# A hybrid recurrent and mixture-of-experts layer on one core: router logits beside the output projection, norms by quarters, the first four experts written out, chunk states on two halves of the rows

## The reference

```python
mod = silu(c) @ ada_w + ada_b                     # six shifts, scales and gates per sequence
h = rmsnorm(x, n1) * (1 + sc1) + sh1
z = h @ w_in                                      # HGRN2 and GLA operands, merge gates ma, mb
o_h, s_h = gated_linear_recurrence(...)           # 4 heads, 128 x 128 state
o_g, s_g = gated_linear_recurrence(...)           # 4 heads, 64 x 128 state
merged = sigmoid(ma) * (o_h @ w_bh) + sigmoid(mb) * (o_g @ w_bg)
x = x + gt1 * (merged @ w_out)
h2 = rmsnorm(x, n2) * (1 + sc2) + sh2
logits = h2 @ r_w + r_b                           # 32 experts, top 4, softmax over these
x = x + gt2 * sum_e combine[:, e] * (swiglu(h2 @ w_gu[e] + b_gu[e]) @ w_dn[e] + b_dn[e])
y = rmsnorm(x, final_g)
```

## Time and profile before

| what | us |
|---|---|
| median of three runs | 1472.11 |
| the profiled execution | 1469.54 |
| its span (first to last instruction) | 1467.5 |
| TensorE matmuls busy | 1311.6 (89%) |
| VectorE / ScalarE / GpSimd busy | 518.3 / 274.4 / 35.1 |
| mean DMA rate over the span | 321 GB/s |
| mean granted TensorE clock | 0.939 of full |

### The profile page before, as it was taken

The page is one execution under the profiler, slowest core; times in us unless marked ns, Lnnn a source line. Parts: engine busy times, 40 slices in busy tenths (PEclk is TensorE's granted clock), DMA queues, the critical chain, the costliest instruction groups (busy, mean ns, idle before and its releaser), DMA issues.

```text
span 1467.5 us, 29078 instructions
## 1 busy us (share of the span) xinstructions
PE 1311.6 (89%) x11811; PEld 595.9 (41%) x11812; DVE 518.3 (35%) x1159; ACT 274.4 (19%) x517; POOL 35.1 (2%) x50
## 2 busy tenths in 40 slices
PE   4999999999978997978787999897999779899996
PEld 1656576666743332323132333232333223243332
DVE  4143334233483332323133344231433223243436
ACT  2130013000011221211011222121222112122222
POOL 0000000000000000000000000000000000000003
PEclk8999999989988999989798999998999989899997
DMA  9877341305275999999999999999799999998830
GB/s 388 311 304 304 113 165 58 117 17 190 83 286 228 409 412 412 416 419 418 419 416 418 418 418 417 416 419 418 283 401 409 411 416 419 418 419 355 328 129 36
DMA packets 87450, 470.92 MB, mean 321 GB/s; under 512 B 7984, under 2 KB 8000, under 8 KB 51360
## 3 DMA queue, kind: packets, MB, share of 16 engines
q1 hardware_dynamic: 84416, 460.68, 77.2%
q0 software_dynamic: 2432, 7.75, 1.9%
q10 hardware_dynamic: 576, 2.11, 0.4%
HBM read 465.66 MB, written 4.85 MB: 321 GB/s over the span
## 4 chain that ended last, share of the span: by engine, by line
PE 72%; DMA 17%; SPq 5%; DVE 3%; issue 2%; ACT 1%; DVEq 0%
PE bank L927 21%; DMA ring<-in_exp_w_dn 12%; PE bank L656 12%; PE bank L944 11%; SPq L451 4%; PE bank L896 4%; PE bank L882 4%; PE bank L793 2%; PE bank L823 2%; PE bank L654 2%; PE bank L903 2%; DMA arena<-in_exp_w_gu 2%; DMA ring<-in_ada_w 2%; DMA ring<-in_exp_w_gu 2%; ACT arena L1178 1%
## 5 line engine op out<-in xcount | busy, mean ns | idle before, releaser
L927 PE MATMUL bank<-arena 128*32 128x512 f32 x1984 | 249.2, 640 | 46.2 <-DMA arena<-in_exp_w_gu 46.0
L944 PE MATMUL bank<-ring,arena 128*32 128x256 f32 x3584 | 219.3, 382 | 33.1 <-ACT arena L1178 18.6
L1621 DVE TENSOR_SCALAR arena<-bank 128x256 f32<-128x256 f32 x56 | 23.8, 425 | 569.2 <-PE bank L927 569.2
L927 PE MATMUL bank<-ring,arena 128*32 128x512 f32 x1600 | 190.8, 622 | 19.0 <-DMA ring<-in_exp_w_gu 19.0
L1615 DVE TENSOR_TENSOR gates<-gates,bank 128x1280 f32<-128x1280 f32 x112 | 166.7, 1488 | 92.7 <-PE bank L896 92.7
L656 PE MATMUL bank<-arena,ring 128*128 128x320 f32 (+1 forms) x592 | 177.4, 461 | 2.7 <-DVE arena L1253 2.0
L944 PEld LDWEIGHTS bank<-ring,arena 128*32 128x32 f32 x3584 | 105.5, 109 | 131.1 <-issue 54.0
L656 PEld LDWEIGHTS bank<-arena,ring 128*128 128x128 f32 (+1 forms) x592 | 117.3, 201 | 66.6 <-issue 25.1
L927 PEld LDWEIGHTS bank<-arena 128*32 128x32 f32 x1984 | 56.3, 112 | 214.3 <-DMA arena<-in_exp_w_gu 106.5
L1175 ACT ACTIVATE arena<-arena 128x256 f32<-128x256 f32 x56 | 23.4, 417 | 459.1 <-DVE arena L1621 459.1
L927 PEld LDWEIGHTS bank<-ring,arena 128*32 128x32 f32 x1600 | 48.3, 112 | 141.8 <-issue 97.7
(11 more groups left out here) (259 smaller groups left out, 926.1 us busy)
## 6 DMA issues: line engine op xcount, KB each, us to landing
ring<-in_exp_w_gu SPq DMA_DIRECT2D x128, 1024.0 KB, 20.2
ring<-in_exp_w_dn SPq DMA_DIRECT2D x128, 1024.0 KB, 11.0
arena<-in_exp_w_gu SPq DMA_DIRECT2D x128, 1024.0 KB, 19.5
ring<-in_ada_w SPq DMA_DIRECT2D x24, 1024.0 KB, 21.1
ring<-in_w_in SPq DMA_DIRECT2D x20, 1024.0 KB, 10.2
ring<-in_w_out SPq DMA_DIRECT2D x4, 1024.0 KB, 7.3
ring<-in_w_in SPq DMA_DIRECT2D x4, 528.0 KB, 10.3
arena<-in_state_hgrn POOLq DMA_DIRECT2D x4, 512.0 KB, 7.8
```

Of the source, the lines that this page charges most:

```text
L927: last = mm(out[part(g), :, :], h2g[:, chunk(k)], w[:, :, columns(g)], start=False, stop=(k == DC - 1), tile_position=(0, CAP * g))
L944: last = mm(banks[2][part(g), HALF:2 * HALF], actT[:, chunk(k)], pair(item_slot(DC + k // 2))[:, k % 2, columns(g)], start=(k == 0), stop= ...
```

## The change

Line numbers of the changed program differ; the names of functions and tiles are kept.

**Chunk states on two halves.** `vmask` has two chunks of columns instead of four. TensorE multiplies rows 0 to 63 and rows 64 to 127 apart, each as a tile of 64 rows, and the two write different banks; `chunk_state(c)` says where chunk `c` is found.

```diff
-                            last = mm(bU[p][p0:p0 + dk, :], kdtok[:, p, p0:p0 + dk],
-                                      vmask[bi][p].rearrange("p c v -> p (c v)"), start=True, stop=True)
+                            for x in range(2):
+                                last = mm(bU[x][p0:p0 + dk, p * 2 * P:(p + 1) * 2 * P], kdtok[64 * x:64 * x + 64, p, p0:p0 + dk],
+                                          vmask[bi][p][64 * x:64 * x + 64, :, :].rearrange("p c v -> p (c v)"),
+                                          start=True, stop=True, tile_position=(64 * x, p0))
```

```diff
+                TS(hT[:, f, 0:TP], xT[:, f, 0:TP], modT[:, 32 + f, 0:1], None, ALU.mult)
+                TT(hT[:, f, TP:T].rearrange("p (b t) -> p b t", t=TSQ), xT[:, f, TP:T].rearrange("p (b t) -> p b t", t=TSQ),
+                   modT[:, 32 + f, 1:NROW].unsqueeze(2).broadcast_to([P, NSEQ, TSQ]), ALU.mult).then_inc(u_scaled, 1)
...
+                if f == 3:
+                    pe.wait_ge(router_landed, 32)
+                    b = open_turn("lsh")
+                    for k in range(DC):
+                        mm(b[0:NROW, 0:E], modT[:, 24 + k, :], rw[:, k, :], start=(k == 0), stop=False)
+                    mm(b[0:NROW, 0:E], ones[0:1, 0:NROW], rb, start=False, stop=True).then_inc(turn_filled, 1)
+                    for n in range(3):
+                        raw_logits(n)
+                elif f > 3:
+                    raw_logits(f - 1)
+            raw_logits(DC - 1)
```

```diff
+            def quarter_sums(b, src, start, stop):
+                for g in range(4):
+                    ins = mm(b[CH * g:CH * g + CH, 0:QT], ones[:, 0:CH], src[:, g * QT:(g + 1) * QT], start=start, stop=stop,
+                             tile_position=(0, CH * g))
...
-            step(nc.vector.reciprocal(r0, r0))
-            dve.wait_ge(router_landed, 32)
-            modulate(32, 24, h2_ready, False)
+            nc.vector.reciprocal(r4, r4).then_inc(r4_ready, 1)
+            wait_filled(dve, "spread3")
+            TT(logT.rearrange("p (g t) -> p g t", g=4), logT.rearrange("p (g t) -> p g t", g=4), upper[0:E, :, 0:QT], ALU.mult)\
+                .then_inc(logits_scaled, 1)
+            for k in range(0, DC, 2):
+                by_quarter = hT[:, k:k + 2, :].rearrange("p k (g t) -> p k g t", g=4)
+                TT(by_quarter, by_quarter, upper[:, :, 0:QT].unsqueeze(1).broadcast_to([P, 2, 4, QT]), ALU.mult)\
+                    .then_inc(h2_scaled, 1)
```

```diff
+            wait_taken(pe, TURN["place"])
+            _, first = nc.values_load_multi_w_load_instructions(itemtab[0:1, 0:5], engines=[mybir.EngineType.PE],
+                                                                min_val=0, max_val=NI - 1)
             pe.wait_ge(comb_ready, 1)
...
-            with pe.Fori(0, E // 4) as fours:
+            for x in range(4):
+                with pe.Fori(first[x], first[x + 1]) as i:
+                    item(i, x // 2, x % 2)
+            with pe.Fori(1, E // 4) as fours:
```

```diff
-            for f in range(6):
-                ins = STT(xT[:, f, :], xT[:, f, :], V("final")[:, f:f + 1], r0, ALU.mult, ALU.mult)
+            for f in range(DC):
+                ins = STT(xT[:, f, :].rearrange("p (g t) -> p g t", g=4), xT[:, f, :].rearrange("p (g t) -> p g t", g=4),
+                          V("final")[:, f:f + 1], lower[:, :, 0:QT], ALU.mult, ALU.mult)
```

More of the change, by code:

```diff
@@ L304, in build @@
         nitems, bounds = rtake(1, 1), rtake(2, 1)
+        assert roff[0] <= 3 * T
+        sq = [rt[:, 3 * T + T * i:4 * T + T * i] for i in range(3)]
+        r4 = small[:, 0:QT]
         posT = small[0:E, 0:T]
@@ L308, in build @@
         frow = rtake(NI, 1)
[L310 removed]
+        lower = ctx.enter_context(nc.psum_tensor("bank0", [P, 4, 512], F32))
         upper = ctx.enter_context(nc.psum_tensor("bank4", [P, 4, 512], F32))
[L312 removed]
+        banks = [lower[:, g, :] for g in range(4)] + [upper[:, g, :] for g in range(4)]
         slot_landed = [sem(f"slot_landed{n}") for n in range(NSLOT)]
@@ L555, in _ @@
                     .then_inc(bdn_landed, 16)
[L557 to L575, removed]
-            pool.wait_ge(added_by_pool, 3)
-            pool.wait_ge(scale3_ready, 1)
-            nc.gpsimd.tensor_tensor(xT[:, 6:8, :], xT[:, 6:8, :], small[:, 0:T].unsqueeze(1).broadcast_to([P, 2, T]), ALU.mult)\
-                .then_inc(y_by_pool, 1)
         @block.tensor
@@ new lines, in _ @@
+            wait_taken(pe, TURN["lsh"])
+            b = open_turn("lflip")
+            for p, (t0, tn) in enumerate(TILES):
+                rows = slice(0, 1) if p < 2 else slice(0, NROW)
+                of_token = ones[0:1, 0:tn] if p < 2 else C("seq9", NROW)
+                mm(b[0:tn, p * E:(p + 1) * E], of_token, lsh[rows, :], start=(p == 0), stop=False, skip_group_check=True)
+            pe.wait_ge(logits_scaled, 1)
+            for p, (t0, tn) in enumerate(TILES):
+                last = mm(b[0:tn, p * E:(p + 1) * E], logT[:, t0:t0 + tn], ident[0:E, 0:E], start=False, stop=True,
+                          skip_group_check=True)
@@ L1009, in _ @@
                 pe.wait_ge(x3sq_ready, n + 1)
-                last = mm(banks[SCATTER[0]][:, 0:T], ones[:, :], hT[:, FEATURES[n], :], start=(n == 0), stop=(n == 7))
+                last = quarter_sums(banks[SCATTER[0]], hT[:, FEATURES[n], :], n == 0, n == 7)
             last.then_inc(ss3_ready, 1)
+            pe.wait_ge(r4_ready, 2)
+            for g in range(4):
+                last = mm(lower[:, g, 0:QT], ident[CH * g:CH * g + CH, CH * g:CH * g + 1].broadcast_to([CH, P]),
+                          r4[CH * g:CH * g + CH, :], start=True, stop=True, tile_position=(CH * g, 0))
+            last.then_inc(scale3_ready, 1)
         @block.scalar
@@ L1196, in _ @@
             act.wait_ge(ss3_ready, 1)
-            A(small[:, 0:T], banks[SCATTER[0]][:, 0:T], ACT.Sqrt, bias=C("eps")).then_inc(root3_ready, 1)
+            A(r4, banks[SCATTER[0]][:, 0:QT], ACT.Sqrt, bias=C("eps")).then_inc(root3_ready, 1)
         @block.vector
```

132 lines of the change are left out of this document (75 added, 57 removed).

## The result

The changed kernel took 1459.69 us (median of 5 runs, 1458.14 to 1466.42), the kernel before, beside it, 1472.11 us (median of 5): a ratio of 0.993, 95% interval 0.9908 to 0.9952, so 12.4 us faster. The predicted time was 1457.6, the range 1450 to 1466.

A forecast was written before the change was run, and what follows sets the result against it. TensorE's instructions bound the recurrences; the experts' 997 us shift as a block. Terms -7.3 - 2.0 - 0.4 - 3.5 = -13.2 from 1469.54 give 1456.3; half of the 2.6 to the median added: 1457.6, range 1450 to 1466.

The forecast's parts named there:

- Chunk states, -7.3: Recurrences on TensorE: two halves overlap, about 1.0 instead of 1.88 us per head, saving 7.3 us; ends 0 and -8.2.
- rival (4): Recurrences: shorter chunk states pull more of the stage to 1.2 GHz, mean clock about 0.84, +23 us, 1480; chance 0.04.
- Rival (1): Chunk states: the halves don't overlap, through mode changes or queueing; that term is 0, time 1465; chance 0.10.
- Routing, -2.0: Output projection and routing: 4.4 us more TensorE work, yet first copy of the logits at 426.9, 2.0 us earlier.
- the rest up to the gather keeps its length: Routing, first copy of the logits to the gather at 435.58: unchanged length, so the gather comes at 433.6.
- ScalarE's line: Routing: ScalarE's shift, table load, exponential and six copies end near 431.3; the gather waits if 2 us of cover fail.
- rival (2): Routing gives nothing back: the projection's +4.4 stays, the term is +2, time 1462; chance 0.15.
- Peeled experts, -0.4: Ahead of the first expert item: moving the load of five numbers saves 0.4 us, between +0.7 and -1.9.
- The end, -3.5: Program end: VectorE takes GpSimd's half, last scalings end at 1460.2 instead of 1463.71, saving 3.5; ends -1.4 and -4.5.
- Rival (3): The end does not get shorter: scalings at 0.69 and a table load no longer covered; time 1460, chance 0.10.
- Two of the signs that I named: Branch projections' end at 376 coming near 368.7, and the first item's products 9 to 10 us before 446.03.

The follow-up runs named there:

- e2: The changed kernel with chunk states as in the kernel before, not on halves: 1467.03 us, ratio 0.9971 to the kernel before.
- e10: The changed kernel with last filling moved, table load behind the items' tables, and unread products in TensorE's routing waits: 1449.40 us, ratio 0.9855 to before.
- e5: The changed kernel with routing and the norm before it as in the kernel before: 1465.13 us, ratio 0.9956 to before.
- e4: The changed kernel with the experts not peeled, the plain loop restored: 1461.30 us, ratio 0.9930 to before.
- e3: The changed kernel itself, measured again with twelve runs: 1464.59 us, ratio 0.9965 to before.
- e6: The changed kernel with the load of the first five numbers moved behind the last products of the items' tables: 1461.68 us, ratio 0.9922 to before.
- e11: The changed kernel with chunk states as before and the last filling moved between the short products: 1466.84 us, ratio 0.9974 to before.
- e12: The kernel before with only the last filling moved between the short products: 1466.70 us, ratio 0.9993 to before.
- e9: The changed kernel with the last filling moved between short products and the table load behind the items' tables: 1452.39 us, ratio 0.9881 to before.

## Why the prediction was right or wrong

The sign holds, and the range holds every median of the changed kernel. But the predicted 1457.6 is 6.7 under the median of its 17 runs, which is as much as the whole gain measured with twelve, and three of the four terms were too good.

**Chunk states, -7.3: mis-sized, -2.4 by the medians (interval 0 to 4.6), nothing in the profiled stage.** The halves do overlap: a group takes 1.06 us to the next instruction, where I expected about 1.0. Two things were wrong in the size. First I set a busy time of 1.88, which holds the tail of the last product, against L748's 1.00 to the next weights; from start to the next product it is 1.71 (127.60 to 129.31 in e2) against 1.06 or 1.07, so 0.65 per head and 5.2 for eight. Second, the clock takes some of these back: about half by the medians, all of it in the profiles, where 0.89 instead of 0.91 in 254 us is 5 us. I had this as rival (4) only in its large form, from a clock of 0.84 on. Its argument against, that fillings of full width follow each group as before, is the step that failed: they follow, and the clock still falls, in the second unit already among the short products ahead of the filling. Why it falls stays open.

The Trainium skill (TensorEngine Tiling, Key Properties) says that a change of tiling mode drains the engine. Eight passes on tiles of 64 rows stand between full ones here and take 1.06 us from their start to the next full product, 0.20 over half of 1.71; that is all the room these rows leave for a drain. Rival (1) is out, though 1465, its time, is near the 17 runs' median: the time is right for another reason.

**Routing, -2.0: -1.2 in the profiled pair.** VectorE begins block 7 at 418.04 (forecast 417.7), and the first copy of the logits comes at 426.67 (forecast 426.9): this chain came out as a whole. One reading in it was wrong: L970's 0.38, which I took for a low clock, is the full one, since the same three products take 0.80 at the low clock (L994 above); the 18 short passes took 0.72 us, not 1.2. What failed is "the rest up to the gather keeps its length": 7.71 us instead of 6.67. I looked for it in ScalarE's line, and the table load does put the exponential 1.46 after the copy, where it was 1.06. But TensorE turns `h2` at 1.2 GHz, 5.28 us instead of 2.84, and the products behind it start only when it ends. e10 shows that this is it: TensorE is kept at work, turns in 2.92, and the choice takes as long as before, with the exponential still 1.46 after the copy. The medians can't tell the term from nothing (e5), but no profile bears rival (2) out: each with the new routing reaches the gather sooner than each with the old one.

**Peeled experts, -0.4: wrong sign, +1.6.** The load's price was right (2.2 forecast, a wait of 2.10), and 0.33 is left for the loop's entry, less than the 0.7 I took. What I missed is the chain behind it: from the positions to the end of VectorE's last copy it is 5.60 us (440.49 to 446.09), where the earlier trace rows give 3.75 (439.34 to 443.09). It runs at the low clock: L1008, the last product of the tables, takes 1.50 us, in e4 (L1005) 1.04. In e3 the clock is full just ahead of the wait (L910 takes 0.37) and low behind it. The wait is not the only way there: in the changed kernel's first profile L910 took 0.62 already ahead of it, and e6 has 1.50 without a wait. The items of the peeled code lie 15.21 instead of 15.28 us apart, but that wins nothing that shows: the tenth waits for weights in every profile, and from the first to the tenth it is 151.6 us in the changed kernel, 152.2 in e3, 152.0 before and 150.4 in e4, which isn't peeled.

**The end, -3.5: right, -3.9.** From the end of the last expert's sum, 1443.17 before (its 1.49 us begin at 1441.68) and 1444.01 after, to the end of the span it is 24.3 and 20.4 us. Eight updates take 3.26 (forecast 3.4), the inverse 0.65 (0.5), eight scalings 3.76 (3.4), and the table load does lie bare between the last square and the root, as forecast. Rival (3) is out.

**The sum.** In the profiled pair the parts close: 0.0 up to the projection, -1.2 to the gather, +1.6 to the first item, +0.4 in the block of experts (997.6 us from 446.42 to 1444.01, before 997.1 from 446.03 to 1443.17) and -3.9 in the end make the -3.1 by which the spans differ. With the -2.4 of the medians for the chunk states it is -5.9, beside the 6.7 measured with twelve runs and the -13.2 of the forecast. Two of the signs that I named did not come: the projection does not begin earlier, and the first item, forecast 9 to 10 us earlier, comes at 446.42 instead of 446.03. The first measurement came within 2.1 of the forecast because its five runs were short, not because the terms were right: the time came out by luck.

## What to carry to other kernels

Where TensorE is busy without a gap, a shorter instruction is worth its length only if the granted clock stays: read the clock per stage before and after, and look at where the dense products stand among runs of short ones, which can be worth more than what was shortened (7 to 8 us here against 2.4, though only together with it). Load registers from a table where products are still queued, ahead of a wait that is there anyway, not on an empty engine. And measure a change of half a per cent with a dozen runs and a second time: five runs gave 12.4 us for what twelve gave as 6.7.

## What the runs showed of the hardware

The granted clock falls without TensorE standing still: 0.89 on average over 254.20 us of which it is busy 252.92. The Trainium skill (TensorE: Matmul & The Clock Gate, Why this matters for your kernels) advises to leave no idle gaps between bursts of products; this stage has 1.28 us of them in all, so the rule doesn't tell where the clock is lost, while in the routing e10's filled waits, with 1.00 granted instead of 0.84, agree with it.

One kernel's runs differ by their clock: over 76 runs of the kernel before, a clock lower by 0.01 goes with 7.4 us. Those runs lie within 12 us. With the filling moved but no halves (e11, e12, twelve runs each) the times spread over 14.6 and 17.7 us, where e9 and e10, with few runs, stay within 2; why is open.
